# A two-layer hybrid decoder on one core: weight units side by side, gate units by their upper input half first, a state product cut by heads

## The reference

```python
def token_mixers(h, ...):
    p = h @ w_in                     # pool, conv GLU a and b, q, k, v, z, decay, beta, three gates
    y_pool = pool_mixer(p[..., pool])                       # window means, then w_pool per group
    y_conv = silu(layer_norm(depthwise31(glu(p)))) @ w_conv_out
    o, S_new = gated_delta_chunked(q, k, v, g, beta, S0)    # per chunk of 64 tokens, 4 heads of 128
    y_dn = gated_rmsnorm(o, z) @ w_dn_out
    mixed = sig(g_A) * y_pool + sig(g_B) * y_conv + sig(g_C) * y_dn
    return mixed @ w_out, ..., S_new

def step(S, xs):                     # one chunk of the delta rule
    vnew = u - w @ S
    o = qg @ S + attn @ vnew
    S = S * g_last + kd.T @ vnew
    return S, o
# each layer: x = LN(alpha*x + token_mixers(x)); x = LN(alpha*x + F(x))
# F: dense SwiGLU (1024 -> 2816 -> 1024) in layer 0, top-2-of-8 experts in layer 1
```

## Time and profile before

| | |
|---|---|
| time, median of 3 runs | 1665.77 us (1664.97 to 1670.49) |
| the profiled execution: time, span | 1667.15 us, 1665.4 us |
| PE busy | 1535.2 us, 92% of the span |
| DVE, ACT, POOL busy | 1089.2 (65%), 811.8 (49%), 491.4 us (30%) |
| mean granted clock of PE | 0.937 of full |
| mixer of layer 0, of layer 1, from the first matmul to the layer norm's sum | 9.57 to 431.05 us, 703.08 to 1130.41 us |

### The profile page before, as it was taken

The page is one execution under the profiler, slowest core; times in us unless marked ns, Lnnn a source line. Parts: engine busy times, 40 slices in busy tenths (PEclk is TensorE's granted clock), DMA queues, the critical chain, the costliest instruction groups (busy, mean ns, idle before and its releaser), DMA issues.

```text
span 1665.4 us, 22890 instructions
## 1 busy us (share of the span) xinstructions
PE 1535.2 (92%) x8707; PEld 1353.6 (81%) x8707; DVE 1089.2 (65%) x1670; ACT 811.8 (49%) x1348; POOL 491.4 (30%) x276
## 2 busy tenths in 40 slices
PE   7999899999799999799998998996999999999995
PEld 6789798887599999778888987974778888888774
DVE  6879795658611011467897956577387877787784
ACT  5645443533333233355454435323466677576673
POOL 0024242000276567300242410011134343343342
PEclk9999898979899999888997989898799999999997
DMA  6322123312355345042222233225377887798780
GB/s 246 124 77 102 52 101 107 127 51 95 114 165 165 119 150 176 1 180 101 98 81 76 77 107 127 72 86 204 111 285 292 328 312 289 263 354 319 271 320 33
DMA packets 57523, 264.66 MB, mean 159 GB/s; under 512 B 9024, under 2 KB 9664, under 8 KB 48448
## 3 DMA queue, kind: packets, MB, share of 16 engines
q1 hardware_dynamic: 57408, 263.11, 44.2%
HBM read 254.54 MB, written 8.54 MB: 158 GB/s over the span
## 4 chain that ended last, share of the span: by engine, by line
PE 39%; DVE 6%; ACT 3%; issue 2%; POOL 1%; POOLq 0%; ACTq 0%; DVEq 0%
PE ps L1340 7%; PE ps L1342 7%; PE ps L1341 7%; PE ps L1288 3%; PE ps L1020 3%; PE ps L1022 2%; PE ps L1021 2%; DVE cacc L1581 1%; DVE Wl L1816 1%; POOL ml L583 1%; ACT mh L901 1%; PE ps L1109 1%; PE ps L1188 1%; PE ps L1227 1%; PE ps L1389 1%
## 5 line engine op out<-in xcount | busy, mean ns | idle before, releaser
L1020 PE MATMUL ps<-Xh,Wl 128*128 128x320 f32 x976 | 336.4, 345 | 25.5 <-DVE Wl L1816 14.2
L1938 DVE TENSOR_TENSOR ml<-mraw,mh 128x1408 fp32r<-128x1408 f32 (+1 forms) x160 | 290.4, 1847 | 76.4 <-ACT mh L901 76.4
L901 ACT ACTIVATE mh<-mraw 128x1408 fp32r<-128x1408 f32 (+1 forms) x216 | 267.9, 1252 | 112.8 <-PE ps L1342 110.3
L1021 PE MATMUL ps<-Xl,Wh 128*128 128x320 f32 x976 | 316.8, 325 | 0.0
L1022 PE MATMUL ps<-Xh,Wh 128*128 128x320 f32 x976 | 316.6, 324 | 0.0
L583 POOL TENSOR_TENSOR ml<-mraw,mh 128x1408 fp32r<-128x1408 f32 (+1 forms) x56 | 178.4, 3185 | 320.5 <-ACT mh L901 320.5
L555 POOL TENSOR_TENSOR cacc<-cacc,G 128x320 f32<-128x320 f32 x120 | 128.9, 1074 | 417.8 <-ACT G L681 408.9
L1020 PEld LDWEIGHTS ps<-Xh,Wl 128*128 128x128 f32 x976 | 197.4, 202 | 49.4 <-issue 29.9
L1816 DVE TENSOR_TENSOR Wl<-raw,Wh 128x1024 fp32r<-128x1024 f32 x138 | 175.6, 1273 | 65.3 <-ACT Wh L610 64.1
L1021 PEld LDWEIGHTS ps<-Xl,Wh 128*128 128x128 f32 x976 | 198.2, 203 | 0.3
L1022 PEld LDWEIGHTS ps<-Xh,Wh 128*128 128x128 f32 x976 | 197.1, 202 | 0.0
(11 more groups left out here) (336 smaller groups left out, 2948.9 us busy)
## 6 DMA issues: line engine op xcount, KB each, us to landing
mraw<-w_moe SPq DMA_DIRECT2D x128, 704.0 KB, 6.5
raw<-w_mix SPq DMA_DIRECT2D x68, 1024.0 KB, 4.7
mraw<-w_moe SPq DMA_DIRECT2D x88, 512.0 KB, 4.7
fraw<-w_ffn SPq DMA_DIRECT2D x44, 512.0 KB, 3.3
fraw<-w_ffn SPq DMA_DIRECT2D x16, 704.0 KB, 3.9
Ss<-st_delta SPq DMA_DIRECT2D x2, 2048.0 KB, 9.0
o_delta_s<-Ss SPq DMA_DIRECT2D x8, 512.0 KB, 2.6
X<-x SPq DMA_DIRECT2D x2, 640.0 KB, 5.5
```

The source lines that it names most:

```text
L901: act.activation(mh[:, n % MS, 0:w], mraw[:, n % MRAW, 0:w], ACT.Copy).then_inc(m_hi, 1)
L1020: pe.matmul(out, wl, xh, start=start, stop=False)
L1021: pe.matmul(out, wh, xl, start=False, stop=False)
L1938: dve.tensor_tensor(ml[:, n % MS, 0:w], mraw[:, n % MRAW, 0:w], mh[:, n % MS, 0:w].bitcast(f32), ALU.subtract).then_inc(m_lod, 1)
```

## The change

1. **Side by side.** Units 0 and 1 go part by part in turn (0, 1, 0, 1, ...), and so do the first three parts of W_out's units 61 and 62, and, per k tile, the FFN's first two units. The weights of units 0 and 1 of layer 0 are both prepared after input tile 3. The new state's products move up: s30 and s31 come before the last two units, and s11 and s20 stand together.
2. **Upper half first.** Units 50 and 51 take tiles 4 to 7 first; after part 3 of unit 51 a new semaphore, `upper_free`, lets `dsplit` go, and both units' lower halves follow. The gaps behind `dsplit` leave the list, so fill comes up to one part later against the chain.
3. **By heads.** p is cut into four pieces of eight matmuls; `ahead` issues heads 0 to 2, each followed by two items of fill. The fill that stood between p, v, o and rs is thereby used up before.
4. **Squares.** ACT's squares 2 and 3 move from `cm` to `cv`.

```diff
 
+        def feed_at(u):
+
+            return 3 if u in (1, U_WO + 1) else 2 if u == U_YP - 2 else 0
+
         def whole(u):
             return [("part", (u, p)) for p in range(4)] + [("unit", u)]
 
-        for u in range(N_QKV):
+        for p in range(4):
+            STEPS += [("part", (0, p)), ("part", (1, p))]
+        STEPS += [("unit", 0), ("qconv", 0), ("unit", 1), ("qact", 0), ("qconv", 1)]
+        for u in range(2, N_QKV):
             quarters = whole(u)
             STEPS += quarters[:2] + ([("ssq", u - 3)] if 3 <= u < 11 else []) + quarters[2:3]
             STEPS += ([("ab", 1)] if u == 5 else []) + quarters[3:]
@@ -376,8 +383,12 @@
 
         fill = []
         for u in range(U_AB, U_YD - 2):
-            if u == U_YP:
-                fill += [("dsplit", 0), ("gap", 0), ("gap", 0)]
+            if u == U_YP - 2:
+                fill += [("part", (v, p)) for v in (u, u + 1) for p in (2, 3)] + [("dsplit", 0)]
+                fill += [("part", (u, 0)), ("part", (u, 1)), ("unit", u), ("part", (u + 1, 0)), ("part", (u + 1, 1)), ("unit", u + 1)]
+                continue
+            if u == U_YP - 1:
+                continue
             if u == U_YC:
                 fill += [("csplit", 0), ("gap", 0)]
@@ -410,6 +421,9 @@
 
         queues = [(fill, len(fill), 0.0, total), (taps, len(taps), 5.0, early), (ptaps, len(ptaps), 6, early)]
         for t, n in CHAIN:
+            if (t, n) == (2, "p"):
+                for h in range(H - 1):
+                    STEPS += [("ahead", h), fill.pop(0), fill.pop(0)]
             STEPS += [("delta", (t, n))]
             if t == 2 and n in ("cv", "t1", "y1", "t2"):
+        STEPS += [("vblk", 0)] + [("part", (U_WO + i, p)) for i in range(2) for p in range(3)]
+        behind = [["s00"], ["s01"], ["s10"], ["s11", "s20"], ["s21"], ["s30"], ["s31"], []]
         for i in range(8):
-            STEPS += ([("vblk", i // 2)] if i % 2 == 0 else []) + whole(U_WO + i) + [("delta", (2, f"s{i // 2}{i % 2}"))]
+            STEPS += ([("vblk", (2, 3, 5).index(i) + 1)] if i in (2, 3, 5) else [])
+            STEPS += whole(U_WO + i)[0 if i > 1 else 3:] + [("delta", (2, n)) for n in behind[i]]
...
             def part(l, u, p):
-                if p == 0 and u < U_WO + 6:
+                if p == feed_at(u) and u < U_WO + 6:
                     head(l * NU + u + 2)
...
             def dsplit(l):
-                act.wait_ge(unit_done, l * NU + U_YP)
+                act.wait_ge(upper_free, l + 1)
...
-                if dict(products(t)).get(name) == "act" or name == "R":
-                    act.wait_ge(dmm, j + 1)
-                inc = consumed(j)[0]
                 if name == "cm":
                     act.wait_ge(z_done, 4 * (l + 1))
-                    for m in range(4):
+                if name in ("cm", "cv"):
+                    for m in ((0, 1) if name == "cm" else (2, 3)):
                         act.wait_ge(ln_cent, ln_at(l, 0) + m + 1)
                         if m >= 2:
                             act.wait_ge(ln_sqs, sqs_at(l, 0) + m - 1)
                         act.activation(sq[:, m % 2, :], cacc[:, m, :], ACT.Square).then_inc(ln_sq, 1)
-                elif name == "cv":
+                if dict(products(t)).get(name) == "act" or name == "R":
+                    act.wait_ge(dmm, j + 1)
+                inc = consumed(j)[0]
+                if name == "cv":
...
                 act.activation(Xh[:, m, :], X[:, m, :], ACT.Copy).then_inc(split_hi, 1)
-                if m % 4 == 3:
-                    head(m // 4)
+                if m == 3:
+                    head(0)
+                    head(1)
...
-                if p == 0:
+                order = (2, 3, 0, 1) if u in (U_YP - 2, U_YP - 1) else (0, 1, 2, 3)
+                first, last = 2 * order[0], 2 * order[3] + 1
+                if p == order[0]:
                     pe.wait_ge(w_lo, n + 1)
...
-                    if p == 0:
+                    if p == order[0]:
                         bank_free(pe, l, g)
...
+                    if (u, p) == (U_YP - 1, 3):
+                        ins.then_inc(upper_free, 1)
...
-                if p == 3:
+                if p == order[3]:
                     ins.then_inc(unit_done, 1)
...
+            def from_state(b, h):
+
+                for i in range(NSEQ):
+                    ins = pe.matmul(b[:, 16 * (8 * h + i):16 * (8 * h + i) + 16], Ss[:, h, i, :],
+                                    wT[:, h, :].rearrange("p (a i n) -> p a i n", a=2, i=NSEQ)[:, :, i, :],
+                                    start=True, stop=True)
+                return ins
+
+            def ahead(l, h):
+
+                j = number(l, 2, "p")
+                if h == 0:
+                    pe.wait_ge(*consumed(j - 4))
+                    pe.wait_ge(*read(l, 2, "w"))
+                    pe.wait_ge(ss_in, 16 * (l + 1))
+                    pe.wait_ge(*read(l, 2, "A"))
+                from_state(dbank(j), h)
...
                 elif name == "p":
-                    pe.wait_ge(*read(l, t, "w"))
-                    pe.wait_ge(ss_in, 16 * (l + 1))
-                    pe.wait_ge(*read(l, t, "A"))
-                    for h in heads:
-                        for i in range(NSEQ):
-                            ins = pe.matmul(b[:, 16 * (8 * h + i):16 * (8 * h + i) + 16], Ss[:, h, i, :],
-                                            wT[:, h, :].rearrange("p (a i n) -> p a i n", a=2, i=NSEQ)[:, :, i, :],
-                                            start=True, stop=True)
+                    ins = from_state(b, H - 1)
...
+                        if i == 0:
+                            continue
+                        if i == 1:
+                            for k in range(KT):
+                                pe.wait_ge(split_lo, split(l, "x1", k))
+                                c = slice(128 * k, 128 * k + 128)
+                                for v in range(2):
+                                    ins = mm3(PS[v][:, 0:T], fh[:, v, c], fl[:, v, c], Xh[:, k, :], Xl[:, k, :],
+                                              k == 0, k == KT - 1)
+                                    if k == KT - 1:
+                                        ins.then_inc(f_done, 1)
+                            continue
                         n, xh, xl = (KT, Xh, Xl) if i < 2 * FT else (FT, Hh, Hl)
                         for k in range(n):
-                            if i == 0:
-                                pe.wait_ge(split_lo, split(l, "x1", k))
...
-                if p == 0 and u < U_WO + 6:
+                if p == feed_at(u) and u < U_WO + 6:
                     wrest(l * NU + u + 2)
...
-                if m % 4 == 3:
-                    wrest(m // 4)
+                if m == 3:
+                    wrest(0)
+                    wrest(1)
```

More of the change, by code:

```diff
@@ L212, in build @@
         ln_std, ln_norm, aff_done, caff_done = sem("ln_std"), sem("ln_norm"), sem("aff_done"), sem("caff_done")
-        yp_seen = sem("yp_seen")
+        yp_seen, upper_free = sem("yp_seen"), sem("upper_free")
         csig, csilu = sem("csig"), sem("csilu")
@@ L1040, in part @@
                         c = slice(128 * k, 128 * k + 128)
-                        ins = mm3(gbank(l, g)[:, 0:T], hi[:, c], lo[:, c], xh[:, k, :], xl[:, k, :], k == 0, k == KT - 1)
+                        ins = mm3(gbank(l, g)[:, 0:T], hi[:, c], lo[:, c], xh[:, k, :], xl[:, k, :], k == first, k == last)
+                    if (u, p) == (U_YP - 1, 3):
+                        ins.then_inc(upper_free, 1)
                 elif u == U_YP:
@@ L1447, in _ @@
                         ln(l, x)
+                    elif kind == "ahead":
+                        ahead(l, x)
                     elif kind == "delta":
```

## The result

The changed kernel takes 1695.25 us (median of four runs, 1686.53 to 1701.32) against 1666.03 (four runs, 1664.97 to 1670.49): ratio 1.0172, 95% interval 1.0144 to 1.0199. It is slower, and the time lies above the range. The profiled execution took 1698.86 us.

The account below looks back on a forecast made before the run. PE, busy 92% of the span, bounds the kernel, so only its idle or half-clock time can be won. 0 - 6.0 - 1.0 + 9.8 + 1.8 - 3.0 = +1.6 us on 1667.15, median 1667.4; range 1654 to 1681.

Parts of the forecast that it names:

- I give back 0.6: Around t1 and x1: one part less of fill stands ahead of each, costing 0.6 us per layer.
- Starts: Side-by-side first units of layers and FFN: 0 us, as the next unit waits for something else; ends -0.4 and +1.7.
- the end of +1.7: Slow end for the starts: longer idle ahead of unit 2 and 3.4 us more at half clock cost 1.7 us.
- Upper half first: Unit 52 and t1, with the squares moved: waits of 2.74 and 0.86 us go; -3.0 us per layer.
- Unit 52 to 53: Unit 52 to unit 53: -0.5 us per layer, with PE idle about 3 us ahead of unit 53.
- p by heads: Unit 53 to rs: cover behind p lost, layer 0's clock loss in both layers; +3.5 and +6.3, sum +9.8 us.
- The loss behind rs: The 24 matmuls behind rs: a third of the half-clock cost, 0.9 us per layer, +1.8 in sum.
- the rival without loss: Unit 53 to rs: clock holds through split p in both layers, 21.5 us each, 1649 us total; chance 0.14.
- that rival's 35.4: Unit 53 to rs all at half clock: 35.4 us per layer, 1678 to 1682 us total; chance 0.17.
- W_out: W_out's new order: shorter wait for `Ml` and less half clock, against new waits; -3.0 us for both layers.
- s20's wait: In W_out, s20 right behind s11 makes PE wait about 1.3 us for `vblk`; +2.6 us in sum.
- The rival about s20: In W_out, s20's wait brings half clock for 3.4 to 6.8 us per layer: 1671 to 1674 us; chance 0.10.

Follow-up runs that it names:

- e10: e5 with one gap in the fill list in place of two; 1676.43 us, ratio 1.0080.
- e5: Changed kernel with both gaps back, p in one block, and W_out's units and state products in the old order; 1656.53 us, ratio 0.9944.
- e12: e5 with p cut by heads, quarters placed between unit 53's parts and behind them, no fill taken from behind p; 1664.12 us, ratio 1.0002.
- e1: Changed kernel with two gaps put back into the fill list behind unit 51; 1668.76 us, ratio 1.0027.
- e9: e5 with squares 2 and 3 back at cm; 1657.34 us, ratio 0.9959.
- e2: Changed kernel with p's 32 matmuls in one block and the fill behind p, v and o as before; 1689.09 us, ratio 1.0173.
- e3: Changed kernel with both gaps back and p in one block; 1661.82 us, ratio 0.9991.
- e6: e3 with each W_out state product behind the unit where it stood before, units 61 and 62 still side by side; 1658.91 us, ratio 0.9957.
- e7: Kernel before with only the upper half first for units 50 and 51 and squares 2 and 3 at cv, both gaps kept; 1658.39 us, ratio 0.9953.

## Why the prediction was wrong, step by step

**The step that failed: a term that the sum does not have.** The working lists starts, upper half, unit 52, p, W_out, and counts the shorter list only where fill stands next to t1 and x1 ("I give back 0.6"). The same shift moves products of both prompt halves and of the samples up to y1. Measured, it costs 10.3 + 8.9 us in the profiled execution and 21 to 30 us in the three pairs of runs that differ by the gaps. The order on PE showed one part less ahead of t1, and the wait for DVE at the first t1 (0.98 us) said that a lacking part of 0.88 us would be added there. The sum over all products could not be had that way, as e10 shows. With 19 more, the sum 1667.4 becomes 1686, below the measured 1695 by the terms that follow.

**Starts: right.** Nothing was won. By unit 16 of layer 0 1.9 us were lost, a little beyond the end of +1.7, and nothing in layer 1; but from the first matmul to unit 16 e5 and e12, which keep the starts, take 82.9 and 82.8 us against 83.1 before, so the starts don't cost this in every execution. The FFN is done with its first two units 1.5 us sooner and waits 1.89 us for `fl` there in place of 0.39, the cover that was named.

**Upper half first: right.** -3.5 and -3.6 against -3.0 (lengths 23.97 to 20.46, and 23.97 to 20.36 in layer 1), and -3.7 with the gaps back (e1). The split of it was off: the squares were given 0.86 us and are worth 2.3 per layer (e9), since without them a wait of 1.36 us for `Wl` comes as well.

**Unit 52 to 53: sized a little short.** -1.4 and -1.2 against -0.5; the idle time ahead of unit 53 is 1.65 us, not 3.

**p by heads: 14.1 us where 9.8 were forecast, but by another way.** The near number is luck: it was to be 3.5 + 6.3 and is 11.4 + 2.8. The loss behind rs, forecast at 1.8, did not come: from unit 55 to 61 both kernels take 25.3 us in either layer. The waits at v, o and rs are 0.94, 0.77 and 1.17 us, 2.9 per layer, where 4 to 5 were expected. In layer 1 they are the whole loss (PE busy for 23.43 us against 23.40): p ran at full clock, and half clock at both ends left a mean of 0.81, between the forecast's 29.9 us and the 21.5 of the rival without loss. Layer 0 was at half clock throughout (mean 0.52, 37.70 us, above that rival's 35.4). The working said that thinning p's matmuls with fill "speaks for a higher clock". That holds where the first quarter began at full clock (layer 1, both layers of e1); in one block p fell to 0.50 from full clock 2.4 to 5.7 us behind its start, in both layers of the kernel before, e2, e3, e5, e6, e7 and e9. Where the clock was low ahead of the first quarter, thinning did not bring it back. What decides whether it is low there stays open: p whole took from 21.7 to 26.5 us for this section in the traces with two gaps. The rule of the Trainium skill, "TensorE: Matmul & The Clock Gate", section "Loop structure matters more than you think", would have kept e12's section at full clock, since PE is back to back there; the trace has 0.50 for 23.8 us, and the measurement decides. In the changed kernel itself PE is not back to back until rs, as the working said beside that page: the three waits stand there.

**W_out: wrong sign.** Forecast -3.0, measured +5.3 (8) by e3 against e5. s20's wait was sized right (1.40 us against 1.3), and so was the wait ahead of the sum (1.61 against 1.6). The 2.63 us wait was to shrink to 1.58 because the two units were read as taking turns; they don't, and it stands. The rival about s20 came true as well: PEclk is 0.50 right behind it for 6.8 us in layer 0 (428.60 to 435.40) and 3.4 us in layer 1 (1138.60 to 1142.00):

```profile
428.60:435.40 6.80, 6.80 (x22) 5.31 (x22) 4.69 (x6) 0.00 (x0) 0.87 (x1) 0.50 0.19 80
1138.60:1142.00 3.40, 3.40 (x12) 2.65 (x11) 3.37 (x6) 0.00 (x0) 0.87 (x1) 0.51 0.02 5
```

## What to carry to other kernels

Where work is dealt into gaps by its share of a list, any item taken from the list, even one that issues nothing, can move everything ahead of it: compare the place of every product before and after, not only of those that the edit names. A product that already waits loses about one filler unit for each that is lacking ahead of it (0.88 us at the first t1), but that gives no sum: here one gap less cost 20 us, as much as two less, and one more cost 16. Check what the slower engine has queued ahead of each result, and time the neighbouring settings. Of this change the upper half first with the squares is worth keeping: with the gaps left in place, p whole and W_out as before (e5) it beats both kernels, by 0.56% (0.43% to 0.69%) against the kernel before.

## What the runs showed of the hardware

Where the granted clock was at 0.50 when they began, matmuls of 16 columns, cut into pieces among matmuls of 320, ran with it at 0.50, for 23.8 us in which PE was never idle (e12). Where it was at 1.00, pieces of that kind ran at 1.00 for 11.5 us (layer 1 of the changed kernel, both layers of e1), while one block of all 32 ended at 0.50 in each of the 14 traced layers named above, the fall coming 2.4 to 5.7 us behind its start. One program's time can also spread widely on one core: the changed kernel ran in 1686.53 us at a mean clock of 0.941 and in 1701.32 at 0.930, and the kernel before in 1656.92 to 1670.02 in the first group. Which stretches change between runs of one program was not looked at, since only one run of each has a trace.
